# PEER gates by indirect word writes into a matrix in memory, in place of one-hot products

## The reference, cut to what matters

```python
v1, i1 = lax.top_k(s1, PEER_TOPK)
v2, i2 = lax.top_k(s2, PEER_TOPK)
cand_s = (v1[..., :, None] + v2[..., None, :]).reshape(b, s, PEER_HEADS, PEER_TOPK * PEER_TOPK)
cand_i = (i1[..., :, None] * N_KEYS + i2[..., None, :]).reshape(b, s, PEER_HEADS, PEER_TOPK * PEER_TOPK)
top_s, pos = lax.top_k(cand_s, PEER_TOPK)
idx = jnp.take_along_axis(cand_i, pos, axis=-1)
gate = jax.nn.softmax(top_s.astype(F32), axis=-1).astype(h.dtype)
...
act = jax.nn.gelu(jnp.einsum('tkd,td->tk', u[ix], hx), approximate=False) * gx
return jnp.einsum('tk,tkd->td', act, v[ix])
```

## Time and profile before

| | |
|---|---|
| time, median of 3 runs | 3869.64 us (3868.07 to 3871.07) |
| span of the profiled execution | 3869.2 us |
| TensorE (PE) busy | 3827.2 us, 99% |
| VectorE (DVE) busy | 2802.9 us, 72% |
| ScalarE (ACT) busy | 1883.7 us, 49% |
| GpSimd (POOL) busy | 1665.4 us, 43% |
| bytes moved by the DMA engines | 875.95 MB, 226 GB/s in the mean |

### The profile page before, as it was taken

One profiled execution on the slowest core, in us unless ns is written; L12 is line 12 of the kernel. 1 busy time (PEld: TensorE's weight loads), 2 busy tenths in 40 slices (PEclk: granted clock), 3 DMA queues, 4 the chain that ended last, 5 costly groups with the idle time before them and its releaser, 6 DMA issues.

```text
span 3869.2 us, 60328 instructions
## 1 busy us (share of the span) xinstructions
PE 3827.2 (99%) x18945; PEld 3308.0 (85%) x18945; DVE 2802.9 (72%) x5195; ACT 1883.7 (49%) x3598; POOL 1665.4 (43%) x1768
## 2 busy tenths in 40 slices
PE   9999999999999999999999999999999999999998
PEld 7665888888888999999788888888888888999997
DVE  4647799778742688887777773999777723888876
ACT  3747433578743333334555553333777723333334
POOL 0311345778730566661200001436887701666641
PEclk9999999999999999999999999999999999999999
DMA  8547566555556899994578773334555566999972
GB/s 276 167 149 196 166 201 204 189 201 196 191 207 201 290 366 361 366 354 153 174 236 244 234 211 108 118 119 142 215 190 189 204 215 206 353 360 366 362 281 93
DMA packets 547287, 875.95 MB, mean 226 GB/s; under 512 B 40592, under 2 KB 384784, under 8 KB 543280
## 3 DMA queue, kind: packets, MB, share of 16 engines
q1 hardware_dynamic: 458688, 605.81, 48.0%
q0 software_dynamic: 51568, 201.04, 14.3%
q10 hardware_dynamic: 36864, 67.13, 4.7%
HBM read 745.57 MB, written 262.21 MB: 260 GB/s over the span
## 4 chain that ended last, share of the span: by engine, by line
PE 91%; ACT 3%; issue 2%; DVE 2%; POOL 1%; DMA 1%; ACTq 0%; DVEq 0%; SPq 0%; POOLq 0%
PE ps L191 83%; PE ps L1771 2%; ACT first_scaled L1790 1%; POOL w_lo L176 1%; PE ps L2314 1%; PE ps L2335 1%; PE ps L1272 1%; PE ps L2085 1%; ACT w_hi L163 1%; PE ps L614 0%; PE ps L615 0%; DMA xbc<-gates 0%; PE ps L600 0%; DVE gate_group L1700 0%; DVE ssd_weights L1122 0%
## 5 line engine op out<-in xcount | busy, mean ns | idle before, releaser
L163 ACT ACTIVATE w_hi<-w_raw 128x1024 fp32r<-128x1024 f32 x692 | 732.7, 1059 | 1194.3 <-PE ps L191 1041.1
L169 DVE TENSOR_TENSOR w_lo<-w_raw,w_hi 128x1024 fp32r<-128x1024 f32 x584 | 718.3, 1230 | 647.7 <-ACT w_hi L163 637.3
L191 PE MATMUL ps<-h_hi,w_hi 128*128 128x512 f32 (+1 forms) x3072 | 1154.1, 376 | 7.7 <-POOL w_lo L176 3.0
L191 PE MATMUL ps<-h_hi,w_lo 128*128 128x512 f32 (+1 forms) x3072 | 1142.1, 372 | 0.0
L191 PE MATMUL ps<-h_lo,w_hi 128*128 128x512 f32 (+1 forms) x3072 | 1141.0, 371 | 0.0
L191 PE MATMUL ps<-y_hi,w_hi 128*128 128x512 f32 (+1 forms) x2368 | 870.0, 367 | 2.0 <-POOL w_lo L176 1.7
L191 PE MATMUL ps<-y_hi,w_lo 128*128 128x512 f32 (+1 forms) x2368 | 867.3, 366 | 0.0
L191 PE MATMUL ps<-y_lo,w_hi 128*128 128x512 f32 (+1 forms) x2368 | 866.9, 366 | 0.0
L191 PEld LDWEIGHTS ps<-h_hi,w_hi 128*128 128x128 f32 x3072 | 577.3, 188 | 97.8 <-issue 11.0
L191 PEld LDWEIGHTS ps<-h_hi,w_lo 128*128 128x128 f32 x3072 | 577.0, 188 | 82.3
L191 PEld LDWEIGHTS ps<-h_lo,w_hi 128*128 128x128 f32 x3072 | 577.5, 188 | 78.0 <-issue 2.1
(11 more groups left out here) (374 smaller groups left out, 3558.3 us busy)
## 6 DMA issues: line engine op xcount, KB each, us to landing
value_rows<-in_v SPq DMA_DIRECT2D x256, 512.0 KB, 6.0
w_raw<-in_u SPq DMA_DIRECT2D x256, 512.0 KB, 3.6
w_raw<-in_v SPq DMA_DIRECT2D x256, 512.0 KB, 5.6
acts<-gelu ACTq DMA_DIRECT2D x256, 256.0 KB, 2.2
gates<-gate_group POOLq DMA_DIRECT2D x28, 2048.0 KB, 8.0
blocks<-acts SPq DMA_DIRECT2D x256, 192.0 KB, 5.2
blocks<-gates SPq DMA_DIRECT2D x96, 512.0 KB, 7.0
w_raw<-in_od_in SPq DMA_DIRECT2D x65, 512.0 KB, 3.6
```

The lines of the kernel that those rows point to most:

```text
L163: self.nc.scalar.activation(self.wh[:, slot % SPL, :], self.raw[:, slot, :], ACT.Copy).then_inc(self.sig("w_hi_ready").sem, 1)
L169: self.nc.vector.tensor_tensor(self.wl[:, slot % SPL, :], self.raw[:, slot, :], self.wh[:, slot % SPL, :].bitcast(F32), ALU.subtract).then ...
L191: ins = self.nc.tensor.matmul(out, a[:, s, w], b[:, k, :], start=first and j == 0 and m == 0, stop=last and j == n - 1 and m == 2)
```

## The change

A matrix of gates for the first 384 tokens lies in memory for each layer (`gate_matrix`: 128 rows for the second key, in each 128 x 384 words for the first key and the token). During TopK ScalarE makes a tile of zeros, and SyncE writes it 24 times, 1 MiB each, over the matrix. Decode computes the place of each pick (`gate_place`, as an integer `gate_at`) and no longer transposes. The new stage Scatter takes the place of Gates and has the same 60 units. In it VectorE computes, for each of 384 columns (a pick of a tile of 128 tokens), the sum of the gates of those of the token's 128 picks that have the same place (`GateMatrix.total`: one 128x128 operation, 8 after each unit), and POOL writes each column of sums to its 128 places by one indirect transfer of 128 words (`GateMatrix.scatter`). Equal places of one token get equal sums; places of different heads of the same tokens are written in order, POOL waiting for the earlier head's 16 transfers of that tile. Values reads the gates of half a block (8 experts' rows, in fours) by one transfer of 768 KB instead of a third of a block by one of 512 KB; SyncE waits for all scattered words after the load of the tail's unit 24 (`GATES_AT`), and reads four halves from there on. The first block's halves are made in the last four units of the tail and no longer in the last eight.

```diff
+class GateMatrix:
+
+
+    TILES = GT // P
+    PIECE = 4
+    EACH = 8
+    WIDE = KEYS * GT
...
+    def clear(self, sp, at):
+
+        n = self.PIECE
+        sp.dma_start(self.rows[:, at].rearrange("p (n t) -> p n t", n=n),
+                     self.none[:, :].unsqueeze(1).to_broadcast([P, n, T])).then_inc(self.zeroed.sem, 16)
+
+    def selection(self, m):
+
+        h, rest = divmod(m, self.TILES * SEL)
+        t, s = divmod(rest, SEL)
+        return h, t, t * P + h * SEL + s
+
+    def total(self, dve, m):
+
+        n, k = self.EACH, self.selection(m)[2]
+        if m % n == 0 and m >= 2 * n:
+            dve.wait_ge(self.totals.sem, self.totals.at(m - n))
+        t = slice(k // P * P, k // P * P + P)
+        self.p.nc.vector.scalar_tensor_tensor(
+            out=self.same[:, m % (2 * n), :], in0=self.place[:, t], scalar=self.place[:, k:k + 1],
+            in1=self.key[:, 2, t], op0=ALU.is_equal, op1=ALU.mult, accum_out=self.sum[:, k:k + 1]
+            ).then_inc(self.totals.sem, 1)
+
+    def scatter(self, pool, m):
+
+        h, t, k = self.selection(m)
+        kept = self.kept[t]
+        if h and m % SEL == 0:
+            pool.wait_ge(kept.sem, kept.at(16 * SEL * h))
+        pool.indirect_dma_start(self.flat, bass.IndirectOffsetOnAxis(ap=self.at[:, k:k + 1], axis=0),
+                                self.sum[:, k:k + 1], None).then_inc(kept.sem, 16)
+
+    def wait_made(self, eng):
+
+        eng.wait_ge(self.zeroed.sem, self.zeroed.at(16 * self.pieces()))
+        eng.wait_ge(self.totals.sem, self.totals.at(GT))
+
+    def wait_kept(self, eng):
+        for m in self.kept:
+            eng.wait_ge(m.sem, m.at(16 * P))
...
@@ TopK.sync
+        m, half = self.matrix, self.matrix.PIECE * T
+        sp.wait_ge(m.none_made.sem, m.none_made.at(1))
+
         def body(n, c, i):
             p.load(sp, i * 8 + u0 + L + 2 * c, (u0 + L + 2 * c) % RAW, us[i * 4 + c, :, :])
+            m.clear(sp, bass.ds(i * (8 * half) + 2 * c * half, half))
             p.load(sp, i * 8 + u0 + L + 2 * c + 1, (u0 + L + 2 * c + 1) % RAW, self.wq[i * 4 + c + L, :, :])
+            m.clear(sp, bass.ds(i * (8 * half) + (2 * c + 1) * half, half))
...
@@ TopK.scalar
         self.norm.act_root(act)
+        self.matrix.make_none(act)
         split(2)
...
@@ Decode.tensor
-        def unit(j):
+        for j in range(self.N):
             self.rows.multiply(pe, n0 + j, (n0 + j) % 2, u0 + j, (u0 + j) % RAW)
-
-        for j in range(self.TURN):
-            unit(j)
-        pe.wait_ge(self.dr.sem, self.dr.at(1))
-        for k in range(3):
-            for t in range(GT // P):
-                ins = p.nc.tensor.transpose(p.ps[:, 2 + k, t * P:(t + 1) * P],
-                                            self.key[:, k, t * P:(t + 1) * P], p.ident[:, :])
-        ins.then_inc(self.dt.sem, 1)
-        for j in range(self.TURN, self.N):
-            unit(j)
...
@@ Decode.vector
-        dve.sem_inc(self.dr.sem, 1)
+        where = matrix.place[:, :].rearrange("p (t s) -> p t s", s=S)
+        side = [key[:, k, 0:GT].rearrange("p (t s) -> p t s", s=S) for k in range(2)]
+        token = p.token[:, 0:GT // P].unsqueeze(2).to_broadcast([P, GT // P, S])
+        link(v.scalar_tensor_tensor(out=where, in0=side[1], scalar=float(KEYS * GT), in1=token, op0=ALU.mult,
+                                    op1=ALU.add))
+        link(v.scalar_tensor_tensor(out=where, in0=side[0], scalar=float(GT), in1=where, op0=ALU.mult,
+                                    op1=ALU.add))
+        link(v.tensor_copy(matrix.at[:, :], matrix.place[:, :]))
...
@@ Scatter
...
+        p, u0, n = self.p, self.u0, self.matrix.EACH
         dve.wait_ge(p.sig("w_lo_ready").sem, u0 + 1)
+        for k in range(self.N):
+            p.split_lo(dve, u0 + k + 1, (u0 + k + 1) % RAW)
+            for m in range(n * k, min(n * k + n, GT)):
+                self.matrix.total(dve, m)
 
     def gpsimd(self, pool):
-        p, TS, Q = self.p, self.TS, self.Q
+        m, n = self.matrix, self.matrix.EACH
+        pool.wait_ge(m.zeroed.sem, m.zeroed.at(16 * m.pieces()))
+        for k in range(GT):
+            if k % n == 0:
+                pool.wait_ge(m.totals.sem, m.totals.at(k + n))
+            m.scatter(pool, k)
 
+        p, u0, n0, UN = self.p, self.u0, self.n0, self.UN
         with pe.Fori(0, self.NS) as g:
             for k in range(UN):
+                self.rows.multiply(pe, g * UN + n0 + k, (n0 + k) % 2, g * UN + u0 + k, (u0 + k) % RAW)
...
@@ Values
     TAIL = 32
     FETCH_AT = 12
-    PIECES = 3
+    GATES_AT = 24
...
+        B, at = BLOCK, self.at
         if again:
             sp.wait_ge(self.al.sem, i * B + self.al.base - 2 * B + j + 1)
         sp.dma_start(at[:, s, j, :], self.rows.acts[bass.ds(i * B + j, 1), :, 0:DT].rearrange("o p t -> (o p) t")
                      ).then_inc(self.bl[s].sem, 16)
-        q = j - (B - self.PIECES)
-        if q >= 0:
-            if again:
-                sp.wait_ge(self.gt_.sem, i * B + self.gt_.base - B)
-            a, c = self.CUTS[q:q + 2]
-            some = self.gates[1 + a:1 + c, :, :].rearrange("g p m -> p g m")
-            sp.dma_start(gt[:, s, a:c, :], some[:, :, bass.ds(i * (B * TG), B * TG)]
-                         ).then_inc(self.bl[s].sem, 16)
+
+    def fetch_gates(self, sp, i, s, j, again):
+
+        B, n = BLOCK, self.QUAD
+        if again:
+            sp.wait_ge(self.gt_.sem, i * B + self.gt_.base - 2 * B + j + n)
+        sp.dma_start(self.gt[:, s, j:j + n, :].rearrange("p j t -> p (j t)"),
+                     self.matrix.rows[:, bass.ds(i * (B * DT) + j * DT, n * DT)]).then_inc(self.bl[s].sem, 16)
...
@@ Values.sync
                 self.rows.wait_stored(sp, self.n0 - 2)
-                for s in range(2):
-                    sp.wait_ge(self.gs.gd[s].sem, self.gs.gd[s].at(16 * (2 * self.gs.NS + 1)))
+                self.matrix.wait_made(sp)
             k = j - self.FETCH_AT
             if 0 <= k < 2 * B:
                 self.fetch(sp, k // B, k // B, k % B, False)
+            if j == self.GATES_AT:
+                self.matrix.wait_kept(sp)
+            k = j - self.GATES_AT
+            if 0 <= k < 4:
+                self.fetch_gates(sp, k // 2, k // 2, k % 2 * self.QUAD, False)
         with sp.Fori(0, NBLOCK // 2 - 1) as ii:
             for k in range(2):
...
                     self.fetch(sp, ii * 2 + k + 2, k, j, True)
+                    if j % self.QUAD == self.QUAD - 1:
+                        self.fetch_gates(sp, ii * 2 + k + 2, k, j + 1 - self.QUAD, True)
...
@@ Values.scalar
-            if k >= self.TAIL - BLOCK:
-                self.his(act, 0, 0, k - self.TAIL + BLOCK)
+            if k >= self.TAIL - 2:
+                for j in range(4 * (k - self.TAIL + 2), 4 * (k - self.TAIL + 3)):
+                    self.hi(act, 0, 0, j)
...
@@ Values.vector
-            if k >= self.TAIL - BLOCK:
-                self.make(dve, 0, 0, k - self.TAIL + BLOCK)
+            if k == self.TAIL - 4:
+                for j in (0, self.QUAD):
+                    self.mult(dve, 0, 0, j)
+            if k >= self.TAIL - 2:
+                self.lo(dve, 0, 0, (k - self.TAIL + 2) * self.QUAD)
```

More of the change, by code:

```diff
@@ L46 @@
 DT = GT
-NTD = DT // TG
-NGD = GT // TG
 NTG = T // TG
@@ L2683, in ffn @@
         with ExitStack() as outer:
[L2684 to L2685 removed]
+            matrix = GateMatrix(p, p.gate_matrix[layer], whole, outer)
             with ExitStack() as ctx:
```

211 lines of the change are left out of this document (48 added, 163 removed).

## The result

The changed kernel takes **3920.3 us** (median of four, 3920.0 to 3920.8), the kernel before 3868.9: ratio 1.0129, 95% interval 1.0116 to 1.0142. So it is slower by 1.3%; forecast were 3914 us and slower. On another chip, where it was timed later, the same kernel took 4437 us, 14.8% more than the kernel before there; that is told further down. First the chip of the result.

A forecast was written before the change was run, and what follows sets the result against it. TensorE, busy 99% of the span, was taken to bound the kernel: 3869.2 - 104.4 + 2 x (70.5 + 3) for wait and clock + 2 for clears, + 100 = 3913.8, given as 3914 us; range 3830 to 3990.

The forecast's parts named there:

- TensorE gains 104.4: Gates and Decode: removing one-hot products and transposes saves TensorE 52.2 us a layer, 104.4 us for both.
- First scatter 726.8, four a unit at 1.36: Scatter stage: POOL starts at 726.8, held by VectorE's low halves to four scatters a unit, 1.36 us each.
- The last 48 at 1.25: End of scattering: with VectorE silent, the last 48 scatters go every 1.25 us, the last issued about 1243.8.
- SyncE let go at 1246.1, TensorE starts at 1254.6: Tail of Values: SyncE's wait for scatters ends at 1246.1; TensorE starts unit 121 at 1254.6.
- the landing of the load: Tail, unit 121's weights: landing takes 3.6 us, after 2.2 us for the gates ahead of them.
- Clock 3 a wait: After TensorE's idle wait in each layer: the lowered clock costs 3 us a wait, between 0 and 5.4.
- Clears 2, of 0 to 20: TopK of layer 0: 24 writes of 1 MiB overfill the DMA engines, costing 2 us of 0 to 20.
- The third rival: TopK of layer 0: clears fill the DMA engines and TensorE waits the whole excess: 3932 us, chance 0.08.
- Rival 1, a POOL at up to 1.29,: Scatter stage: POOL is quicker, 1.25 us a scatter gives 3840, up to 1.16 gives 3767; chance 0.23.
- Rival 2, words that drain slowly,: Scatter stage: words drain slower than issued and hold POOL; 1.6 us a scatter gives 4105; chance 0.17.
- the landing of the scatters: End of scattering, before SyncE's wait ends: scattered words land 3.5 us after their issue.
- the wait's own sum: Tail, before unit 121: scatter end, gate reads, load and halves add to a TensorE wait of 70.5 us a layer.

The follow-up runs named there:

- quarters: Changed kernel with VectorE's low half of units 36 to 127 made in four operations of 256 columns instead of one of 1024: 4468.6 us on chip B.
- The version with all edits: Changed kernel with gate reads on POOL's queue, low halves in four pieces and an earlier scatter start: 3797.6 us, ratio 0.9815 to the kernel before.
- the pair of kernels on A: Changed kernel with gate reads moved to POOL's queue, 3859.0 us; the same plus low halves in four pieces and an earlier scatter start, 3797.6 us.

## Why the prediction was right, and what it missed

1. *TensorE gains 104.4.* Right: it gains 103.6, and without the wait the span is 3766.2, 103.0 under the one before. The transposes gave 1.0 a layer for 1.2, and 1.0 is lost in the mixer of layer 1.
2. *First scatter 726.8, four a unit at 1.36.* 728.13; 336 issued before 1184, as worked out; 1.36 to within 0.003. The reason holds too (quarters, and no long scatters without low halves). The Trainium skill (SBUF — State Buffer, Who interferes with whom) has, in the sentence that the prediction took, that two-input operations did not stall such transfers; here it is 0.97 against 1.83, and the traces do not agree. The same section also says that such an operation contends with a GpSimd instruction that reads SBUF. A scatter reads its places there, so that sentence, which the prediction left aside, agrees with the traces.
3. *The last 48 at 1.25.* 1.27: a scatter is 0.967 long where the gather was 0.94. Last one 1244.8 against 1243.8.
4. *SyncE let go at 1246.1, TensorE starts at 1254.6.* 1247.0 and 1257.5. The sum has a slip: 1243.8 + 3.5 is 1247.3, which would have made the wait 71.7 and the total 3916. It did little harm because the landing was taken too long: SyncE was let go 2.2 us after the last scatter's start, and not 3.5. The mis-sized term is the landing of the load behind a read of gates: 7.6 us where I summed 2.2 and 3.6. The sum has nothing for POOL's gathers of value rows, which start 1.3 us behind the last scatter; how much of the 1.8 us is theirs no run shows. The wait was 73.8 and 73.4 for 70.5.
5. *Clock 3 a wait.* 2.4 and 2.8 for unit 121.
6. *Clears 2, of 0 to 20.* Nothing: TensorE is busy throughout TopK in both layers, and the clears by themselves make no difference. The third rival falls: its overload was there (1.05), but its depth is what counts, and it stayed below the 24 us of lead.
7. *Rival 1, a POOL at up to 1.29,* fell: it was 1.36. The version with all edits comes near it, at 1.30, but its gain of 72 us also needs the earlier start and the reads on POOL's queue.
8. *Rival 2, words that drain slowly,* fell on the chip of the result. On B and C the time is further off than that rival had it (4437 for 4105), and its mechanism is still wrong: the words do not drain slower. None of my cases had scatters slow down other engines' instructions, no row of the trace before could have shown it, and by that measure the range holds for one sort of chip only.

The forecast was thus right by its own steps for the chip that was measured, and 523 us short on another. That it came within 7 us owes something to small errors that cancel: the clears, the clock and the landing of the scatters were taken too long, the landing of the load and the wait's own sum too short. No run on a chip like A has the low half made twice, in quarters alone, or left out; the lock rests on the fit of 764 scatters, on the pair of kernels on A, and on the lengths of the scatters on B and C.

## What to carry to other kernels

A wait costs what is queued behind it on its engine: put a wait for a slow producer on a queue that has nothing else to feed, here POOL's own, and not on the one that loads the weights. A sequence of short indirect transfers is paced by how long the single VectorE operations beside it are, more than by how much VectorE does: cutting them brought 1.36 down to 1.30, of at best 1.27. And a change that brings in a new kind of traffic should be timed on more than one chip before its percent is believed.

## What was not expected of the hardware

- On two chips, instructions of TensorE and VectorE come 0.7 to 2.8 us apart, for the most part in steps of 0.70, while POOL scatters words to memory; on the chip of the result they don't. 4437 us against 3920 for the same kernel. The cause is open.
- A scatter of 128 words that begins inside a two-input VectorE operation ends 0.84 us after it (the gathers: 0.82); free, it takes 0.967, with 0.30 to the next. Without low halves of 1.22 us beside them, 1 of 768 is over 1.1 us; with them, 66 of 768 on the same chip.
- Word writes cost the DMA engines nearly nothing: 1.7% of their time at one scatter in 1.36 us.
